# Sums of squares in four column tiles, root and reciprocal on a quarter of the width, and weights split in one piece of 1024 columns

## The chip, the cores and the metric

The kernel runs on one core of a Trainium2 chip. The time is that of the device for one execution, in microseconds (us); before the change it is 1908.05 us, the median of three runs (1899.71 to 1910.66). PE is the matrix engine, DVE the vector engine, ACT the scalar engine, POOL the GpSimd engine and SP the engine that issues the weight transfers.

## The reference, cut to what matters

Two layers work on 528 tokens (512 and 16 meta tokens) of 1024 channels. Each has a token mixer and a channel mixer, and an RMS norm stands before each of them:

```python
def rmsnorm(x, g):
    x32 = x.astype(jnp.float32)
    y = x32 * lax.rsqrt(jnp.mean(x32 * x32, axis=-1, keepdims=True) + EPS)
    return (y * g.astype(jnp.float32)).astype(x.dtype)

for layer in range(DEPTH):                 # DEPTH = 2
    hn = rmsnorm(hs, mix_norm[layer])      # norm 0 (layer 0), norm 2 (layer 1)
    z = hn @ w_in[layer]                   # then the S5 and RG-LRU branches, gates, w_out
    ...
    hn = rmsnorm(hs, ffn_norm[layer])      # norm 1 (layer 0), norm 3 (layer 1)
    # layer 0: dense SwiGLU of 3072 hidden channels; layer 1: top 2 of 8 experts
```

## The kernel before

Activations stand transposed: 128 partitions carry channels, tile `m` of 8 carries channels 128m to 128m+127, and the free axis carries the 528 tokens. Every product is made of three products of float32r halves (high times high, high times low, low times high). Weights arrive in units of 128 x 1024 float32. For the mixers and the dense part (164 units, the "ring" of three buffers `raw`, `wh`, `wl`) SP loads a unit in two halves of 512 columns (`HALVES`), ACT copies each half to `wh` (the high part, L683), DVE subtracts to get `wl` (the low part, L1052), and PE runs 48 matmuls on the unit (`unit`, L1578). The expert part has its own buffers (`mraw`, `mwh`, `mwl`), always in pieces of 1024 columns, and is not touched. Each engine runs its own list in the order in which the code is written; engines wait for each other by semaphores only.

A norm is spread over the engines. ACT squares tile m (`square`, L696). PE multiplies the squares with a 128 x 128 matrix of ones (`add_squares`, L1586), in full float32, so that the sum over channels stands on all 128 partitions of the PSUM tile `side`; each such matmul shows as two records. For norms 1, 2 and 3 `add_squares` of a tile stands between the units of the product before, two tiles late, and the last two stand at its end. Then, in `norm`, ACT loads the table of the square root with a one-column instruction into `warm` (L700), takes the root of all 528 columns into `rs` (L702), DVE takes the reciprocal in place (L1070), and for each tile DVE multiplies `hs`, the norm's weight and `rs` (L1078), ACT makes `xh`, DVE makes `xl`, and PE starts `first_units` (L1608), two weight units interleaved, tile by tile. Norm 3 feeds the router instead (L1780); PE transposes `hs` (L1765) meanwhile. In norms 0 and 2 POOL prepares tables of the S5 branch at the same time; the first of them, `m1t` (L572), is waited for by PE at L1652.

Of the kernel before, what the change touches and what calls it, by code (L numbers as in the profile page):

```python
# [71 lines left out]
RING = 3  # L72
HALVES = ((0, slice(0, UNIT // 2)), (1, slice(UNIT // 2, UNIT)))
U_IN = 28
# [21 lines left out]
def build(nc, xT, W, cols_d, s5p, s5m, wg, rw, rb, fg, out, hs_d, u_d, y_d, xg_d, yg_d):  # L96
    ctx = ExitStack()
    with ctx:
# [24 lines left out]
        def sem(name):  # L123
            return ctx.enter_context(nc.semaphore(name))
# [171 lines left out]
        side_free = [sem("side_free0"), sem("side_free1")]  # L296
        raw_landed = [[sem(f"raw_landed{i}_{h}") for h in range(2)] for i in range(RING)]
        hi_ready = [sem(f"hi_ready{i}") for i in range(RING)]
# [4 lines left out]
        const_ready = sem("const_ready")  # L303
        hs_ready, sq_ready, ss_ready, rms_ready = sem("hs_ready"), sem("sq_ready"), sem("ss_ready"), sem("rms_ready")
        hn_ready, xh_ready, xl_ready = sem("hn_ready"), sem("xh_ready"), sem("xl_ready")
        hs_saved, hs_back = sem("hs_saved"), sem("hs_back")
# [55 lines left out]
        def live(l, x):  # L362

            return x[:, META:T] if l else halves(x)

        def summed(l, pair):

            return pair[:, 0, 0:TR] if l else pair[:, :, 0:TH]
# [48 lines left out]
        def _(sp):  # L417
# [3 lines left out]
            for u in range(RING):  # L421
                for h, cs in HALVES:
                    sp.dma_start(raw[u][:, cs], W[u, :, cs]).then_inc(raw_landed[u][h], 16)
            with sp.Fori(1, UNITS // RING) as it:
                for s in range(RING):
                    for h, cs in HALVES:
                        sp.wait_ge(lo_ready[s], it * 2 + (h - 1))
                        sp.dma_start(raw[s][:, cs], W[it * RING + s, :, cs]).then_inc(raw_landed[s][h], 16)
            for u in range(UNITS // RING * RING, UNITS):
                s, n = use(u)  # L430
                for h, cs in HALVES:
                    sp.wait_ge(lo_ready[s], 2 * n + h - 1)
                    sp.dma_start(raw[s][:, cs], W[u, :, cs]).then_inc(raw_landed[s][h], 16)
            sp.wait_ge(tab_ready2, 1)
# [230 lines left out]
        def _(act):  # L665
# [8 lines left out]
            def split_hi(u, more=0):  # L674

                if isinstance(u, int) and isinstance(more, int) and u + RING * more >= UNITS:
                    return
                s, n = use(u, more)
                if u >= RING:
                    act.wait_ge(unit_done[s], n)  # L680
                for h, cs in HALVES:
# [8 lines left out]
            def square(i, m):  # L690
# [5 lines left out]
                a.activation(hn[:, m, span], hs[:, m, span], ACT.Square).then_inc(sq_ready, 1)  # L696

            def norm(i):
# [62 lines left out]
            def mixer(l):  # L761
# [94 lines left out]
                for m in range(DK):  # L856
                    act.dma_start(hs[:, m, :], (hs_d if l else xT)[:, m, :]).then_inc(hs_back, 16)
                for m in range(DK):
# [19 lines left out]
            def down(u0, e, last):  # L878
                more = e * (U_FF // RING)
                for j in range(FT):  # L880
# [161 lines left out]
        def _(dve):  # L1042
# [11 lines left out]
            def split_lo(u, more=0):  # L1054
                if isinstance(u, int) and isinstance(more, int) and u + RING * more >= UNITS:
                    return
                s, n = use(u, more)
                for h, cs in HALVES:
# [7 lines left out]
            def norm(i):  # L1066
                name, layer = (("mix_norm", 0), ("ffn_norm", 0), ("mix_norm", 1), ("ffn_norm", 1))[i]
                dve.wait_ge(rms_ready, i + 1)
                span = slice(META if i == 3 else 0, T)
                link(v.reciprocal(rs[:, span], rs[:, span]))  # L1070

# [484 lines left out]
        def _(pe):  # L1556
# [7 lines left out]
            def unit(u, jobs, more=0, before=None, sums=None, short=False):  # L1564
# [3 lines left out]
                s, n = use(u, more)  # L1568
                pe.wait_ge(lo_ready[s], n * 2 + 2)
                for n, (k, a, hi, lo, first, last) in enumerate(jobs):  # L1570
# [11 lines left out]
            def add_squares(i, m):  # L1582

                pe.wait_ge(sq_ready, i * DK + m + 1)
                for b, (t0, t1) in enumerate(((META, T),) if i == 3 else ((0, TH), (TH, T))):
                    ins = mm(side[:, b, 0:t1 - t0], ones[:, :], hn[:, m, t0:t1],  # L1586
                             start=m == 0, stop=m == DK - 1)
                if m == DK - 1:
                    ins.then_inc(ss_ready, 1)

            def norm(i):
                if i == 0:
                    pe.wait_ge(const_ready, 1)
                    for m in range(DK):
                        add_squares(i, m)

            def first_units(u, split):

                slots = [use(u + a) for a in range(2)]
                for s, n in slots:  # L1600
                    pe.wait_ge(lo_ready[s], n * 2 + 2)
                for k in range(DK):
# [155 lines left out]
            for l in range(LAYERS):  # L1758
                if l:
# [10 lines left out]
                    for t in range(TB):  # L1770
                        if t == 1:
                            pe.wait_ge(rms_ready, 4)
                        if t >= 2:
                            pe.wait_ge(hs_tok_ready, t - 1)
                        rows_of(hs, t, 1 - t % 2)

                    pe.wait_ge(prep_pool, 16 * 2)
# [249 lines left out]
```

## Time and profile before

| | |
|---|---|
| median of three runs | 1908.05 us |
| the profiled execution | 1904.79 us |
| its span | 1903.3 us |
| mean granted clock of PE, share of full | 0.952 |
| PE busy | 1741.2 us, 91% |
| DVE busy | 1038.6 us, 55% |
| ACT busy | 789.5 us, 41% |
| POOL busy | 469.0 us, 25% |

The span runs from the first to the last instruction. Busy shares are means over stages with different limits. Times in the rows are microseconds from the start of the span; a row of the timeline joins instructions of one kind that stand together and gives their count. PE's granted clock has two levels, 2.4 GHz (1.0) and 1.2 GHz (0.5).

### The profile page before, as it was taken

The numbers are of one execution on the slowest core, as the hardware profiler recorded it, in microseconds if no ns is written. First come the engines' busy times: TensorE is split into PE (matmuls) and PEld (weight loads), VectorE is DVE, ScalarE is ACT, GpSimd is POOL, SyncE is SP. The second block draws the span as 40 slices with busy tenths as digits, with TensorE's granted clock in tenths as the row PEclk, the third lists the DMA queues.
The fourth block names the chain that finished last, engine by engine and source line by source line (L and its number), as shares of the span: only waits on it lengthen the run. The fifth ranks groups of instructions, "written<-read, shape, count | busy, mean of one in ns | idle before, by whom it ended". The sixth has DMA issues, their size and how long they took to land.

```text
span 1903.3 us, 29292 instructions
## 1 busy us (share of the span) xinstructions
PE 1741.2 (91%) x10884; PEld 1556.1 (82%) x10884; DVE 1038.6 (55%) x1453; ACT 789.5 (41%) x1128; POOL 469.0 (25%) x1201
## 2 busy tenths in 40 slices
PE   4799998998999999998898898996999999999993
PEld 4688998998999999998786786875888877877882
DVE  5556553645333233325366545626855766866885
ACT  4234424323222122223343425224744765765773
POOL 5876783002000000003658881001000000000001
PEclk8788998999999999999888999998999999999997
DMA  3521222246322222223512122314975986986994
GB/s 119 105 60 50 60 79 69 81 141 258 114 92 89 89 89 88 88 89 110 112 57 64 59 78 65 113 66 183 412 252 175 338 301 206 343 304 211 347 367 175
DMA packets 123834, 290.28 MB, mean 153 GB/s; under 512 B 31024, under 2 KB 31152, under 8 KB 123584
## 3 DMA queue, kind: packets, MB, share of 16 engines
q1 hardware_dynamic: 90576, 241.38, 36.0%
q0 software_dynamic: 9120, 32.02, 4.7%
q10 hardware_dynamic: 24016, 15.25, 3.8%
q8 instruction: 77, 1.26, 0.3%
q14 instruction: 45, 0.37, 0.1%
HBM read 260.09 MB, written 28.51 MB: 152 GB/s over the span
## 4 chain that ended last, share of the span: by engine, by line
PE 76%; DVE 9%; ACT 5%; issue 5%; DMA 3%; ACTq 2%; SPq 0%; POOL 0%; POOLq 0%; DVEq 0%
PE acc L1578 40%; PE acc L1820 7%; PE acc L1821 7%; PE acc L1822 7%; PE side L1578 2%; PE side L1662 2%; PE acc L1818 2%; PE acc L1819 1%; PE acc L1608 1%; ACTq L827 1%; DMA uu<-u_d 1%; ACT wh L683 1%; PE side L1586 1%; DVE rs L1070 1%; PE side L1866 1%
## 5 line engine op out<-in xcount | busy, mean ns | idle before, releaser
L1578 PE MATMUL acc<-xh,wh 128*128 128x264 f32 (+1 forms) x1600 | 384.0, 310 | 8.2 <-DVE wl L1052 3.8
L1052 DVE TENSOR_TENSOR mwl<-mraw,mwh 128x1024 fp32r<-128x1024 f32 x288 | 337.6, 1220 | 72.5 <-ACT mwh L947 71.7
L1578 PE MATMUL acc<-xl,wh 128*128 128x264 f32 (+1 forms) x1600 | 375.4, 305 | 0.0
L1578 PE MATMUL acc<-xh,wl 128*128 128x264 f32 (+1 forms) x1600 | 373.6, 304 | 0.0
L1052 DVE TENSOR_TENSOR wl<-raw,wh 128x512 fp32r<-128x512 f32 x328 | 217.9, 705 | 268.5 <-ACT wh L683 263.8
L947 ACT ACTIVATE mwh<-mraw 128x1024 fp32r<-128x1024 f32 x288 | 288.3, 1053 | 61.7 <-PE acc L1822 32.3
L1578 PEld LDWEIGHTS acc<-xh,wh 128*128 128x128 f32 x1600 | 262.7, 193 | 29.2 <-issue 13.8
L1578 PEld LDWEIGHTS acc<-xl,wh 128*128 128x128 f32 x1600 | 261.6, 192 | 10.3 <-issue 1.2
L1578 PEld LDWEIGHTS acc<-xh,wl 128*128 128x128 f32 x1600 | 260.8, 192 | 10.2
L683 ACT ACTIVATE wh<-raw 128x512 fp32r<-128x512 f32 x328 | 187.4, 621 | 188.2 <-PE acc L1578 144.5
L1820 PE MATMUL acc<-mwh,xth 128*128 128x512 f32 x432 | 171.1, 396 | 8.4 <-ACT ytok L1013 5.4
L1822 PE MATMUL acc<-mwl,xth 128*128 128x512 f32 x432 | 168.8, 391 | 0.0
L1821 PE MATMUL acc<-mwh,xtl 128*128 128x512 f32 x432 | 168.8, 391 | 0.0
L639 POOL DMA_DIRECT2D yg_d<-ytok x11 | 5.9, 541 | 522.7 <-ACT ytok L1013 519.1
L534 POOL DMA_DIRECT2D gw<-in_wg x4 | 2.2, 565 | 428.0 <-DVE hs L1267 427.7
L1820 PEld LDWEIGHTS acc<-mwh,xth 128*128 128x128 f32 x432 | 81.5, 189 | 28.0 <-issue 11.2
L1822 PEld LDWEIGHTS acc<-mwl,xth 128*128 128x128 f32 x432 | 81.4, 188 | 17.4
L1821 PEld LDWEIGHTS acc<-mwh,xtl 128*128 128x128 f32 x432 | 81.5, 189 | 16.4
L1820 PE MATMUL acc<-mwh,hth 128*128 128x512 f32 x216 | 85.9, 398 | 0.0
L1821 PE MATMUL acc<-mwh,htl 128*128 128x512 f32 x216 | 84.2, 390 | 0.0
L1822 PE MATMUL acc<-mwl,hth 128*128 128x512 f32 x216 | 84.2, 390 | 0.0
L1578 PE MATMUL acc<-fh,wh 128*128 128x264 f32 x384 | 79.3, 288 | 0.0
(379 smaller groups left out, 2943.3 us busy)
## 6 DMA issues: line engine op xcount, KB each, us to landing
mraw<-in_W SPq DMA_DIRECT2D x288, 512.0 KB, 5.4
raw<-in_W SPq DMA_DIRECT2D x328, 256.0 KB, 2.7
xg_d<-zero POOLq DMA_DIRECT2D x15, 512.0 KB, 9.9
yg_d<-ytok POOLq DMA_DIRECT2D x9, 512.0 KB, 3.7
xt<-xg_d POOLq DMA_DIRECT2D x8, 512.0 KB, 8.6
yg_d<-zero POOLq DMA_DIRECT2D x5, 512.0 KB, 20.1
hs<-in_xT SPq DMA_DIRECT2D x8, 264.0 KB, 4.7
u_d<-uperm ACTq DMA_DIRECT2D x8, 264.0 KB, 2.1
```

What stands on the lines that cost most here:

```text
L683: a.activation(wh[s][:, cs], raw[s][:, cs], ACT.Copy).then_inc(hi_ready[s], 1)
L827: act.dma_start(y_d[b * GB:(b + 1) * GB, :, j, :].rearrange("g h c -> h g c"), ys[j * GC:(j + 1) * GC, b % 2, :, :]).then_inc(y_out[b % 2] ...
L947: a.activation(mwh[w][:, :], mraw[j % RAWS][:, :], ACT.Copy).then_inc(wide_hi[w], 1)
L1052: return v.tensor_tensor(out, a, b, op)
L1070: link(v.reciprocal(rs[:, span], rs[:, span]))
L1578: ins = mm(out, w, x[:, t0:t1], start=first and i == 0, stop=last and i == 2)
L1586: ins = mm(side[:, b, 0:t1 - t0], ones[:, :], hn[:, m, t0:t1], start=m == 0, stop=m == DK - 1)
L1662: ins = mm(out4, ident[:, at:at + P], taps[:, :].rearrange("p (g h) -> p g h", g=GB), start=True, stop=True)
L1818: ins = mm(out[0:HALF], hi[:, 0:HALF], mwl[w][:, cols], start=False, stop=False)
L1820: mm(out, hi, mwh[w][:, cols], start=first, stop=False)
L1821: mm(out, lo, mwh[w][:, cols], start=False, stop=False)
L1822: return mm(out, hi, mwl[w][:, cols], start=False, stop=last)
```

## The change

Three things change in the norms. The sums of squares of a tile are no longer made by two matmuls of 264 tokens on all 128 columns of the array, but by four matmuls of 132 tokens with 32 columns of ones each: quarter g of the tokens goes to partitions 32g to 32g+31. Root and reciprocal then work on 132 columns instead of 528. A new step, `spread_inverse`, brings quarter g of the reciprocals back to all partitions with a full-array float32 matmul whose 128 weight columns are all the unit vector of row 32g; its result stands in PSUM, and L1078's multiplication reads it from there. The load of the root's table moves ahead: to the start of the last stretch of units before norms 1, 2 and 3. For norm 3 the quarters are of 128 tokens, and the new matmuls stand after the first of PE's four groups of transposes.

The fourth thing is the split of the ring's units: transfer, high part and low part of a unit are one instruction of 1024 columns each, with one semaphore each.

```diff
-HALVES = ((0, slice(0, UNIT // 2)), (1, slice(UNIT // 2, UNIT)))
...
+        def quarter(i):
+
+            return (T - span_of(i)) // 4
+
+        def spread(i):
+
+            w = 2 * quarter(i)
+            return acc[:, 0, 1, 0:2 * w].rearrange("p (b c) -> p b c", b=2) if i == 3 else side[:, 2:4, 0:w]
...
                 for s in range(RING):
-                    for h, cs in HALVES:
-                        sp.wait_ge(lo_ready[s], it * 2 + (h - 1))
-                        sp.dma_start(raw[s][:, cs], W[it * RING + s, :, cs]).then_inc(raw_landed[s][h], 16)
+                    sp.wait_ge(lo_ready[s], it)
+                    sp.dma_start(raw[s][:, :], W[it * RING + s, :, :]).then_inc(raw_landed[s], 16)
...
-                for h, cs in HALVES:
-                    act.wait_ge(raw_landed[s][h], n * 16 + 16)
-                    a.activation(wh[s][:, cs], raw[s][:, cs], ACT.Copy).then_inc(hi_ready[s], 1)
+                act.wait_ge(raw_landed[s], n * 16 + 16)
+                a.activation(wh[s][:, :], raw[s][:, :], ACT.Copy).then_inc(hi_ready[s], 1)
...
             def norm(i):
-                act.wait_ge(const_ready, 1)
-                a.activation(warm[:, :], ones[:, 0:1], ACT.Sqrt)
+                if i == 0:
+                    act.wait_ge(const_ready, 1)
+                    sqrt_table()
                 act.wait_ge(ss_ready, i + 1)
-                a.activation(live(i == 3, rs[:, :]), summed(i == 3, side[:, 0:2, :]), ACT.Sqrt, scale=1.0 / D, bias=EPS)\
+                w = quarter(i)
+                a.activation(rs[:, 0:w], side[:, 0, 0:w], ACT.Sqrt, scale=1.0 / D, bias=EPS)\
...
-                for h, cs in HALVES:
-                    dve.wait_ge(hi_ready[s], n * 2 + (h + 1))
-                    tt(wl[s][:, cs], raw[s][:, cs], wh[s][:, cs].bitcast(F32), ALU.subtract).then_inc(lo_ready[s], 1)
+                dve.wait_ge(hi_ready[s], n + 1)
+                tt(wl[s][:, :], raw[s][:, :], wh[s][:, :].bitcast(F32), ALU.subtract).then_inc(lo_ready[s], 1)
...
-                link(v.reciprocal(rs[:, span], rs[:, span]))
+                span, w = slice(span_of(i), T), quarter(i)
+                v.reciprocal(rs[:, 0:w], rs[:, 0:w]).then_inc(inv_ready, 1)
+                dve.wait_ge(spread_ready, i + 1)
...
-                    v.scalar_tensor_tensor(out=hn[:, m, span], in0=hs[:, m, span], scalar=g, in1=rs[:, span],
+                    v.scalar_tensor_tensor(out=halves(hn[:, m, span]), in0=halves(hs[:, m, span]), scalar=g, in1=spread(i),
...
-                for b, (t0, t1) in enumerate(((META, T),) if i == 3 else ((0, TH), (TH, T))):
-                    ins = mm(side[:, b, 0:t1 - t0], ones[:, :], hn[:, m, t0:t1],
+                w = quarter(i)
+                for g in range(4):
+                    t0 = span_of(i) + g * w
+                    ins = mm(side[32 * g:32 * g + 32, 0, 0:w], ones[:, 0:32], hn[:, m, t0:t0 + w],
                              start=m == 0, stop=m == DK - 1)
...
+            def spread_inverse(i):
+
+                w = quarter(i)
+                pe.wait_ge(inv_ready, i + 1)
+                for g in range(4):
+                    ins = mm(spread(i)[:, g // 2, g % 2 * w:(g % 2 + 1) * w],
+                             ident[:, 32 * g:32 * g + 1].to_broadcast([P, P]), rs[:, 0:w], start=True, stop=True)
+                ins.then_inc(spread_ready, 1)
```

ACT's list from the last stretch of the dense part to norm 2, before the change (`wh<-raw` is a unit's high part, `hn<-hs` the square of a tile, `rs<-side` the root):

```order
L866 COMPARE_AND_BRANCH
L683 ACTIVATE wh_57<-raw_54 128x512 x2
...
L885 DMA hs_d<-hs 128x3696
L696 ACTIVATE hn<-hs 128x528
L914 DMA hs_d<-hs 128x528
L700 ACT_TABLE_LOAD
L700 ACTIVATE warm<-ones 128x1
L702 ACTIVATE rs<-side 128x528
L708 ACTIVATE xh<-hn 128x528 x8
```

And the same place after it:

```order
L883 COMPARE_AND_BRANCH
L710 ACT_TABLE_LOAD
L710 ACTIVATE warm<-ones 128x1
L693 ACTIVATE wh_57<-raw_54 128x1024
...
L904 DMA hs_d<-hs 128x3696
L706 ACTIVATE hn<-hs 128x528
L933 DMA hs_d<-hs 128x528
L718 ACTIVATE rs<-side 128x132
L724 ACTIVATE xh<-hn 128x528 x8
```

The table load and the one-column instruction moved from between the last square and the root to a place eight units earlier; the root has 132 columns, and a unit's high part is one instruction.

PE's list at norm 3, before the change (L1578 is the last unit, L1765 the transposes of `hs`, L1780 the router's product):

```order
L1578 MATMUL acc<-xl,wh_58 128x512
L1578 MATMUL acc<-xh,wl_61 128x512
L1586 MATMUL side<-hn,ones 128x512 x3
L1765 MATMUL side<-ident,hs 128x128 x32
L1780 MATMUL acc<-hn,rws 8x512 x8
L1784 MATMUL acc<-ident,lgt 128x8 x4
```

And after it (L1626 is `spread_inverse`):

```order
L1597 MATMUL acc<-xh,wl_61 128x512
L1607 MATMUL side<-hn,ones 32x128 x12
L1798 MATMUL side<-ident,hs 128x128 x8
L1626 MATMUL acc<-rs,ident 128x128 x4
L1798 MATMUL side<-ident,hs 128x128 x24
L1815 MATMUL acc<-hn,rws 8x512 x8
```

The three full-array matmuls on the squares became twelve of 32 columns, and the spreading matmuls stand between the first eight transposes and the other 24, which now wait behind them.

## Rows read from the trace of the kernel before

**Rows 1.** The page's part 4: shares of the chain that ended last, by engine.

```profile
PE 76%; DVE 9%; ACT 5%; issue 5%; DMA 3%; ACTq 2%; SPq 0%; POOL 0%; POOLq 0%; DVEq 0%
```

**Rows 2.** Waits of PE: line, waited for: us in total, times, longest.

```profile
PE acc L1608 <- DVE xl L1052: 24.9, 3, 11.7
```

**Rows 3.** Timeline of norm 1: start, length, engine, line, operation, count, idle before.

```profile
444.23 0.64 ACT L696 ACTIVATE hn<-hs 128x528 f32<-128x528 f32 x1 [5.79 <-DVE hs L1231]
444.89 1.28 ACT L700 ACT_TABLE_LOAD   x1
446.30 0.59 ACT L702 ACTIVATE rs<-side 128x528 f32<-128x528 f32 x1
446.92 3.45 DVE L1070 RECIPROCAL rs<-rs 128x528 f32<-128x528 f32 x1 [2.72 <-ACT rs L702]
450.41 1.45 DVE L1078 SCALAR_TENSOR_TENSOR hn<-hs,cols,rs 128x528 f32<-128x528 f32 x2
443.30 2.83 PE L1586 MATMUL side<-hn,ones 128*128 128x264 f32 x12
452.74 0.78 PE L1608 MATMUL acc<-xh,wh 128*128 128x264 f32 x2 [6.62 <-DVE xl L1052]
```

**Rows 4.** Timeline: short forms on DVE and ACT, full-array float32 on PE.

```profile
19.41 0.55 DVE L1295 RECIPROCAL p_rden<-p_den 128x64 f32<-128x64 f32 x1
69.99 0.22 ACT L806 ACTIVATE taps<-side 128x64 f32<-128x64 f32 x1 [4.87 <-PE side L1652]
1140.17 1.99 PE L1662 MATMUL side<-taps,ident 128*128 128x64 f32 x16
```

**Rows 5.** Timeline of PE: two sums of squares between two units.

```profile
868.88 1.05 PE L1586 MATMUL side<-hn,ones 128*128 128x264 f32 x4
870.01 0.40 PE L1578 MATMUL acc<-fl,wh 128*128 128x264 f32 x2
```

**Rows 6.** Timeline of PE at the tiled matmuls L1624, and their weight loads.

```profile
100.50 0.39 PE L1685 MATMUL side<-sr,m2y 128*128 128x66 f32 x2
100.82 1.11 PE L1624 MATMUL side<-xc,gw 64*64 64x264 f32 x8
101.86 0.51 PE L1578 MATMUL acc<-xh,wh 128*128 128x264 f32 x2
102.21 0.41 PE L1578 MATMUL acc<-xl,wh 128*128 128x264 f32 x2
L1624 PEld LDWEIGHTS side<-xc,gw x128: 129/133/228, 100.8 to 1058.2; 64*64 64x64 f32 x128
```

**Rows 7.** Windows (span, busy PE, PEld, DVE, ACT, POOL, clock); timeline of POOL, PE.

```profile
30.10:42.00 11.90, 9.38 (x65) 9.41 (x66) 11.87 (x19) 5.96 (x10) 10.66 (x17) 0.76 0.01 2
43.40:54.50 11.10, 8.68 (x70) 8.26 (x68) 10.38 (x51) 5.92 (x8) 9.13 (x27) 1.00 0.34 113
120.94 0.29 POOL L476 TENSOR_TENSOR pt<-cfi,pbuf 128x64 f32<-128x64 f32 x1
68.09 1.86 PE L1652 MATMUL side<-c,m1t 128*128 128x16 f32 x8 [4.13 <-issue]
```

**Rows 8.** Timeline of PE at the router.

```profile
1291.58 7.03 PE L1780 MATMUL acc<-hn,rws 128*8 128x512 f32 x16 [0.97 <-DVE hn L1078]
```

**Rows 9.** The chain of waits; two stalls of PE in the timeline.

```profile
452.74 13.22 PE acc L1608 x96
410.65 5.85 PE acc L1578 x48
128.34 0.69 PE L1683 MATMUL side<-uu,m 128*128 128x66 f32 x2 [2.44 <-DVE sr L1052]
163.21 0.44 PE L1683 MATMUL side<-uu,m 128*128 128x66 f32 x2 [2.46 <-DVE sr L1052]
```

**Rows 10.** The page's part 5: DVE's low parts in both sizes.

```profile
L1052 DVE TENSOR_TENSOR mwl<-mraw,mwh 128x1024 fp32r<-128x1024 f32 x288 | 337.6, 1220 | 72.5 <-ACT mwh L947 71.7
L1052 DVE TENSOR_TENSOR wl<-raw,wh 128x512 fp32r<-128x512 f32 x328 | 217.9, 705 | 268.5 <-ACT wh L683 263.8
```

More of the change, by code:

```diff
@@ L296, in build @@
         side_free = [sem("side_free0"), sem("side_free1")]
-        raw_landed = [[sem(f"raw_landed{i}_{h}") for h in range(2)] for i in range(RING)]
+        raw_landed = [sem(f"raw_landed{i}") for i in range(RING)]
         hi_ready = [sem(f"hi_ready{i}") for i in range(RING)]
@@ L304, in build @@
         hs_ready, sq_ready, ss_ready, rms_ready = sem("hs_ready"), sem("sq_ready"), sem("ss_ready"), sem("rms_ready")
+        inv_ready, spread_ready = sem("inv_ready"), sem("spread_ready")
         hn_ready, xh_ready, xl_ready = sem("hn_ready"), sem("xh_ready"), sem("xl_ready")
@@ L364, in live, with span_of @@
             return x[:, META:T] if l else halves(x)
+        def span_of(i):
+            return META if i == 3 else 0
+        def quarter(i):
[3 more added lines that the diff above has]
+            return acc[:, 0, 1, 0:2 * w].rearrange("p (b c) -> p b c", b=2) if i == 3 else side[:, 2:4, 0:w]
         def summed(l, pair):
@@ L421, in _ @@
             for u in range(RING):
-                for h, cs in HALVES:
-                    sp.dma_start(raw[u][:, cs], W[u, :, cs]).then_inc(raw_landed[u][h], 16)
+                sp.dma_start(raw[u][:, :], W[u, :, :]).then_inc(raw_landed[u], 16)
             with sp.Fori(1, UNITS // RING) as it:
                 for s in range(RING):
-                    for h, cs in HALVES:
-                        sp.wait_ge(lo_ready[s], it * 2 + (h - 1))
-                        sp.dma_start(raw[s][:, cs], W[it * RING + s, :, cs]).then_inc(raw_landed[s][h], 16)
+                    sp.wait_ge(lo_ready[s], it)
+                    sp.dma_start(raw[s][:, :], W[it * RING + s, :, :]).then_inc(raw_landed[s], 16)
             for u in range(UNITS // RING * RING, UNITS):
                 s, n = use(u)
-                for h, cs in HALVES:
-                    sp.wait_ge(lo_ready[s], 2 * n + h - 1)
-                    sp.dma_start(raw[s][:, cs], W[u, :, cs]).then_inc(raw_landed[s][h], 16)
+                sp.wait_ge(lo_ready[s], n)
+                sp.dma_start(raw[s][:, :], W[u, :, :]).then_inc(raw_landed[s], 16)
             sp.wait_ge(tab_ready2, 1)
@@ L696, in square, with sqrt_table @@
                 a.activation(hn[:, m, span], hs[:, m, span], ACT.Square).then_inc(sq_ready, 1)
+            def sqrt_table():
+                a.activation(warm[:, :], ones[:, 0:1], ACT.Sqrt)
             def norm(i):
-                act.wait_ge(const_ready, 1)
-                a.activation(warm[:, :], ones[:, 0:1], ACT.Sqrt)
+                if i == 0:
+                    act.wait_ge(const_ready, 1)
+                    sqrt_table()
                 act.wait_ge(ss_ready, i + 1)
-                a.activation(live(i == 3, rs[:, :]), summed(i == 3, side[:, 0:2, :]), ACT.Sqrt, scale=1.0 / D, bias=EPS)\
+                w = quarter(i)
+                a.activation(rs[:, 0:w], side[:, 0, 0:w], ACT.Sqrt, scale=1.0 / D, bias=EPS)\
                     .then_inc(rms_ready, 1)
@@ L857, in mixer @@
                     act.dma_start(hs[:, m, :], (hs_d if l else xT)[:, m, :]).then_inc(hs_back, 16)
+                sqrt_table()
                 for m in range(DK):
@@ L879, in down @@
                 more = e * (U_FF // RING)
+                if last:
+                    sqrt_table()
                 for j in range(FT):
@@ L1068, in norm @@
                 dve.wait_ge(rms_ready, i + 1)
-                span = slice(META if i == 3 else 0, T)
-                link(v.reciprocal(rs[:, span], rs[:, span]))
+                span, w = slice(span_of(i), T), quarter(i)
+                v.reciprocal(rs[:, 0:w], rs[:, 0:w]).then_inc(inv_ready, 1)
+                dve.wait_ge(spread_ready, i + 1)
                 def lower(m):
@@ L1568, in unit @@
                 s, n = use(u, more)
-                pe.wait_ge(lo_ready[s], n * 2 + 2)
+                pe.wait_ge(lo_ready[s], n + 1)
                 for n, (k, a, hi, lo, first, last) in enumerate(jobs):
@@ L1592, in norm @@
                 if i == 0:
-                    pe.wait_ge(const_ready, 1)
+                    pe.wait_ge(const_ready, 2)
                     for m in range(DK):
                         add_squares(i, m)
+                if i == 3:
+                    return
+                spread_inverse(i)
+            def spread_inverse(i):
[5 more added lines that the diff above has]
+                ins.then_inc(spread_ready, 1)
             def first_units(u, split):
@@ L1600, in first_units @@
                 for s, n in slots:
-                    pe.wait_ge(lo_ready[s], n * 2 + 2)
+                    pe.wait_ge(lo_ready[s], n + 1)
                 for k in range(DK):
@@ L1775, in _ @@
                         rows_of(hs, t, 1 - t % 2)
+                        if t == 0:
+                            spread_inverse(3)
                     pe.wait_ge(prep_pool, 16 * 2)
```

2 lines of the change are left out of this document (removed).

## The prediction

> **What bounds the kernel now.** I read the chain of waits first: 76% of it is PE, 9% DVE, 5% ACT [rows 1]. So an edit pays where it shortens PE's own list or a stretch in which PE stands still. The waits of PE come next: the longest sum is the first weight units after norms 0 to 2 waiting for DVE's `xl`, 24.9 us in three times [rows 2]. The timeline of norm 1 shows that wait's inside [rows 3]: PE's last sum of squares ends at 443.30 + 2.83 = 446.13 and PE works again at 452.74. Between them stand the rest of the table load, the root (0.59), the reciprocal (3.45, the largest piece), the first multiplications and splits. The reader is to see that all of it is one after the other. The change aims at two places: this stretch, and the sums of squares in PE's list. The split of the ring's units touches ACT and DVE, which mostly wait.
>
> **The stretch in norms 1 and 2.** I go through norm 1; norm 2 has the same list.
> - Table load: it ends at 446.17, and the root follows. The last square ends at 444.87 [rows 3]. Moved ahead, the load costs ACT 1.28 us earlier, covered by idle time such as the 5.79 us before that square; without that cover it would delay one high part by 1.5 us, with nearly two units (5.85 us each, [rows 9]) until PE needs it. The root then waits for the last sums alone. They start at about 444.92, and I give them 0.44 us of steps and 0.28 us of run-out, so the root starts at 445.65 instead of 446.30: -0.65.
> - Root: 0.22 us for 64 columns from PSUM [rows 4], 0.59 for 528 [rows 3]; on the line between them 132 columns take 0.28: -0.31.
> - Reciprocal: 0.55 us for 64 columns [rows 4], 3.45 for 528, so 6.25 ns a column and 0.98 for 132: -2.47.
> - Spreading, which is new and entirely on the path: four full-array float32 matmuls, eight records. Sixteen records of 64 columns took 1.99 us with their run-out, 0.12 each [rows 4]; records of 264 columns come 0.22 apart (four in 1.05 with run-out, [rows 5]). A record of 132 columns has half of the latter's work, 0.11, so the 0.12 of the former counts: 8 x 0.12 = 0.96, and 0.24 for run-out and the two handovers: +1.20. At half clock it would be +2.1.
> - The multiplication reads PSUM instead of SBUF: counted as nothing.
>
> Sum: -2.2 us each, -4.4 for both. The bounds are -1.3 (half clock) and -2.4.
>
> **Norm 0.** PE has been idle there long, so the spreading costs +2.1 and DVE gains only about 0.7 us. What ends last is another thing: PE reaches the S5 branch's first matmul and waits 4.13 us until 68.09 for POOL's table [rows 7]. POOL is slowed by DVE: between 30.10 and 42.00, with DVE in two-operand work from SBUF, it did 17 operations in 11.9 us (0.70 each); between 43.40 and 54.50, 27 in 11.1 us (0.41) [rows 7]. The 17 lost 17 x 0.29 = 4.9 us to 16 large DVE operations, 0.3 each. While DVE multiplied a PSUM operand with one from SBUF, at 120.94, POOL's operation took 0.29 us, its undisturbed length [rows 7]. The eight multiplications of the norm now have their second operand in PSUM, so POOL gains 8 x 0.3 = 2.4 us, and the 4.13 us of waiting can give that. Bounds: 0 and 4.1. I take -2.4. The Trainium skill ("SBUF — State Buffer", in the list of port rules) says that a DVE operation with two SBUF inputs and a GpSimd operation that reads SBUF exclude each other for the whole instruction. The trace agrees with it in the 0.29 us against 0.70. Without it, the first mixer would get norm 0's 0.7 us at most, and the sum would be 1.7 us less.
>
> **Norm 3.** The router's product waits 0.97 us for DVE [rows 8]; that is all that the shorter root and reciprocal can give. The spreading matmuls stand before three groups of transposes that were done under the reciprocal and now come behind it. I take -0.3; bounds -1.0 and +1.0.
>
> **Sums of squares in PE's list.** Of 24 (eight each for norms 1 to 3), 21 stand in PE's stream, three in the stretches above. One costs now: from 868.88 to the second pair of the next unit at 870.01, less one pair's step of 0.24, is 0.89 us [rows 5]. The new one has eight records of 132 columns, 0.11 us of work each. How many run at once no row shows for this form. The nearest is the gate product on tiles of 64 x 64: eight records of 264 columns (0.22 each) took from 100.82 to 101.86, 1.04 us, where one after the other would be 1.76: two at a time. Around them the neighbours stand 0.10 further apart on each side (100.50 to 100.82 for 0.22; 101.86 to 102.21 for 0.25) [rows 6]. So 0.88 us are work and 0.36 are the cost of going to tiles and back. Two at a time, the new form costs 0.44 + 0.36 = 0.80; four at a time 0.22 + 0.36 = 0.58; one at a time 0.88 + 0.36 = 1.24. I take the middle of the first two, 0.69, because there are four tiles here: -0.20 each, -4.2 in all. Bounds: -6.5 and +7.4, and worse if the weight loads count too (below).
>
> **The split in one piece.** Per unit DVE spends 1.22 us instead of two of 0.705, and ACT similarly less [rows 10], but both wait for PE most of the time. Where the split stands in DVE's or ACT's part of the chain (about eight places in the mixers, by the chain of waits) it saves 0.1 us: -0.8. Against it: the low part can only start when the whole high part is done, so the pair ends 0.4 us later where DVE waits. PE's slack of nearly two units covers that; if none did, the eight places would cost +3. A transfer of 512 KB lands later than its first half did; that matters only where a transfer is late.
>
> **Sum.** -4.4 - 2.4 - 0.3 - 4.2 - 0.8 = -12.1 us, against the profiled execution's 1904.79 (span 1903.3, the rest is around it): 1892.7. That execution is one of four, whose median is 1906.4; the three shown have 1908.05. From 1906.4 the sum gives 1894.3. I forecast **1894 us**.
>
> **Rivals.**
> - *More than that* (1889): four tiles at a time give 2.3 us more, and the clock holds. After the stretch of norm 1 the first 96 matmuls take 13.22 us where 96 at full clock take 2 x 5.85 = 11.70 [rows 9]: 1.5 us lost, 3 in two norms. With matmuls in its middle the quiet time falls to about 2.4 us. For it speaks a stall of 2.46 us after which the records have full-clock length (0.44 for two), against it one of 2.44 us after which they have 0.69 [rows 9]. So it is open, and I leave it out of the sum.
> - *The norms' own stretches only* (1901): POOL's gain is lost to another wait before 68.09 or behind it, and a sum of squares costs what it did: 4.4 + 0.3 + 0.8 = 5.5 us of gain. Free waits in the mixers between ACT, DVE and POOL speak for it.
> - *The tiling does not do what it says* (1906): tiles run one after another. 21 x 0.35 = 7.4 us are lost and the other 7.9 gained. Rows 6 speak for pairs only, and cannot tell which two records run together.
> - *Slower: weight loads in line* (1928). If a column tile's load waits for the matmul before it, since all four tiles use all rows, each record costs its load too: 0.13 us [rows 6]. Then a sum of squares takes 8 x 0.24 + 0.36 = 2.28 us, 1.39 more than now, 29 us in 21 places, against 7.9 gained: 1906.4 + 21.3. It decides from 1.27 us for one sum of squares. Against it: in [rows 6] eight loads of 0.13 and eight records of 0.22 took 1.04 us, so loads were hidden, but there the tiles differ in rows. The Trainium skill ("TensorE: Matmul & The Clock Gate", Part 3) says that a weight load overlaps a running matmul only if the row group differs. No run so far shows it for column tiles. The same page reports a gain of 2.38 times for three column tiles, which by itself speaks for the case of several at a time.
>
> **How the numbers follow.** Chances: the forecast 0.41, more 0.20, norms only 0.22, tiles in line 0.09, loads in line 0.08. The measurement tells 0.5% from no change, that is 1898.5 or less against 1908.05. The forecast has its own range of 1888 to 1900 and counts 0.8 as faster, the first rival wholly, the second 0.3: 0.33 + 0.20 + 0.07 = 0.60 faster. Slower are the last rival and a rest: 0.08. The remaining 0.32 is within 0.5%. The range, 1882 to 1907, takes in all but the last rival and the tails.
>
> **What would show it.** Right: a reciprocal of about 1 us; PE back at work 2.2 us sooner after its last sums in norms 1 and 2; the first matmul on POOL's table about 2.4 us earlier than 68.09; a sum of squares that costs PE 0.6 to 0.8 us between units. Wrong: one of 1.2 us or more; spreading matmuls of over 2 us; PE waiting for a unit's low part in the mixers; longer half-clock stretches there.

## The result, and the profile after

The changed kernel takes 1888.48 us (median of eight runs, 1879.06 to 1894.03) where the kernel before, run beside it, takes 1905.72 (eight runs, 1896.55 to 1910.66): a ratio of 0.991, interval 0.9891 to 0.9929, or about 17 us. A second set of runs gave 0.9919 (0.990 to 0.9937), 15 us. The forecast was 1894 with a range of 1882 to 1907. The direction and the range held; the terms behind the sum did worse, as the traces show. The measured median lies on the 1889 of the rival called "more than that".

The profiled execution took 1883.83 us, its span 1882.3 against 1903.3. The page's share of the chain that ended last, by engine, answers to [rows 1]:

```profile
PE 73%; DVE 6%; issue 5%; ACT 5%; POOL 4%; DMA 3%; ACTq 2%; SPq 0%; POOLq 0%; DVEq 0%
```

PE's waits (line, what it waited for: us in total, times, longest) answer to [rows 2]. Before, PE stood 12.5 us for the last squares (the first row below is of the kernel before) and 24.9 for `xl`. The 24.9 are now two pieces, one for the quarter reciprocal and one for the first `xl`; the wait for the squares stays. Norm 0 has the longest wait for the squares and the longest for the reciprocal.

```profile
PE side L1586 <- ACT hn L696: 12.5, 2, 11.9
PE side L1607 <- ACT hn L706: 15.4, 4, 12.6
PE side L1626 <- DVE rs L1088: 13.8, 3, 11.0
PE acc L1641 <- DVE xl L1071: 7.2, 3, 2.4
PE side L1716 <- DVE sr L1071: 7.8, 6, 2.8
```

The timeline of norm 1 (start, length, engine, line, operation, count, idle before) answers to [rows 3]:

```profile
432.20 0.64 ACT L706 ACTIVATE hn<-hs 128x528 f32<-128x528 f32 x1 [5.55 <-DVE hs L1250]
432.90 0.43 PE L1607 MATMUL side<-hn,ones 128*32 128x132 f32 x8 [0.88 <-ACT hn L706]
433.40 0.28 ACT L718 ACTIVATE rs<-side 128x132 f32<-128x132 f32 x1 [0.55 <-PE side L1607]
433.71 0.98 DVE L1088 RECIPROCAL rs<-rs 128x132 f32<-128x132 f32 x1 [1.54 <-ACT rs L718]
434.75 2.13 PE L1626 MATMUL side<-rs,ident 128*128 128x132 f32 x8 [1.41 <-DVE rs L1088]
436.91 1.44 DVE L1097 SCALAR_TENSOR_TENSOR hn<-hs,cols,side 128x528 f32<-128x528 f32 x2 [2.22 <-PE side L1626]
439.24 0.78 PE L1641 MATMUL acc<-xh,wh 128*128 128x264 f32 x2 [2.37 <-DVE xl L1071]
```

The root and the reciprocal have the forecast lengths to the hundredth (0.28, 0.98). The spreading takes 2.13 us, not 1.2.

A sum of squares between two units, and its weight loads, answer to [rows 5]:

```profile
855.17 0.43 PE L1607 MATMUL side<-hn,ones 128*32 128x132 f32 x8
855.88 0.40 PE L1597 MATMUL acc<-fl,wh 128*128 128x264 f32 x2
L1607 PEld LDWEIGHTS side<-hn,ones x256: 106/109/154, 12.5 to 1264.3; 128*32 128x32 f32 x128
```

By the same reckoning as for [rows 5] it costs 855.88 - 855.17 - 0.24 = 0.47 us, where it was 0.89. The eight records span 0.43 us, the last one's run-out with them. With 0.11 us of work each and a length of about 0.28, two at a time would span 0.6; one after the other on the full array such records span 1.06 (sums_full below). So four ran at a time.

Where did the 21.0 us between the two traces come from? Windows of the two kernels over the same stages (span, then busy time and count of PE, PEld, DVE, ACT and POOL, clock, DMA share, GB/s). Before, the first mixer up to the last wait for `y1l`, then the second mixer:

```profile
32.62:327.14 294.52, 262.46 (x1953) 252.82 (x1953) 165.21 (x311) 104.99 (x172) 213.37 (x571) 0.89 0.27 70
891.82:1169.39 277.57, 248.19 (x1472) 215.41 (x1473) 148.76 (x237) 104.59 (x172) 195.38 (x518) 0.92 0.27 72
```

After, the same:

```profile
32.36:317.16 284.80, 254.80 (x1952) 245.98 (x1953) 156.96 (x283) 102.11 (x144) 221.26 (x573) 0.94 0.28 73
875.91:1150.40 274.49, 248.56 (x1473) 216.18 (x1473) 140.80 (x209) 101.84 (x144) 202.09 (x521) 0.92 0.28 73
```

| stage | before | after | less |
|---|---|---|---|
| norm 0 and start | 32.62 | 32.36 | 0.3 |
| first mixer to the wait for `y1l` | 294.52 | 284.80 | 9.7 |
| rest of it, with eight sums of squares | 118.99 | 116.17 | 2.8 |
| norm 1, from the last sum to the first unit | 6.61 | 5.91 | 0.7 |
| dense part, with eight sums | 432.41 | 430.71 | 1.7 |
| norm 2 | 6.67 | 5.96 | 0.7 |
| second mixer to `y1l` | 277.57 | 274.49 | 3.1 |
| rest, norm 3, router | 144.13 | 141.77 | 2.4 |
| experts to the end | 589.78 | 590.13 | -0.3 |

The profiled execution is the second fastest of its eight, 4.6 us under their median, so the 21.0 us are more than the 15 to 17 of the medians.

The largest piece lies where the prediction had only POOL's gain. In the first mixer PE did the same instructions (1953 and 1952), yet was busy 7.7 us less: a granted clock of 0.94 in place of 0.89 (about 0.01 of that is a stretch that the record misses, see the last section). Only 2.1 us less are idle. So three questions were open: what the split and the norms give apart, what the clock does to both, and how much of this stage is chance.

### The profile page after: what moved, and what is told of

The parts are those of the page before. It is cut to its first block, busy times and chain, and to the rows that moved or that the text cites. A ratio compares the mean times of both kernels' runs of the same rounds, so it can differ in the third digit from the quotient of the medians.

```text
span 1882.3 us, 28818 instructions
## 1 busy us (share of the span) xinstructions
PE 1728.1 (92%) x11060; PEld 1541.1 (82%) x11060; DVE 1006.2 (53%) x1289; ACT 772.4 (41%) x964; POOL 481.2 (26%) x1201
## 4 chain that ended last, share of the span: by engine, by line
PE 73%; DVE 6%; issue 5%; ACT 5%; POOL 4%; DMA 3%; ACTq 2%; SPq 0%; POOLq 0%; DVEq 0%
PE acc L1597 38%; PE acc L1855 7%; PE acc L1856 7%; PE acc L1857 7%; PE side L1597 2%; PE acc L1853 2%; PE side L1695 2%; PE acc L1854 2%; PE acc L1641 1%; ACTq L843 1%; DMA mraw<-in_W 1%; DMA uu<-u_d 1%; POOL pt L487 1%; ACT wh L693 1%; PE side L1901 1%
## 5 line engine op out<-in xcount | busy, mean ns | idle before, releaser
L1597 PE MATMUL acc<-xh,wh 128*128 128x264 f32 (+1 forms) x1600 | 379.9, 307 | 5.4 <-DVEq L1253 2.2
L1071 DVE TENSOR_TENSOR wl<-raw,wh 128x1024 fp32r<-128x1024 f32 x164 | 203.5, 1242 | 299.6 <-ACT wh L693 298.9
L693 ACT ACTIVATE wh<-raw 128x1024 fp32r<-128x1024 f32 x164 | 172.2, 1051 | 178.1 <-PE acc L1597 142.5
```

What stands on the lines that cost most here:

```text
L693: a.activation(wh[s][:, :], raw[s][:, :], ACT.Copy).then_inc(hi_ready[s], 1)
L1071: return v.tensor_tensor(out, a, b, op)
L1597: ins = mm(out, w, x[:, t0:t1], start=first and i == 0, stop=last and i == 2)
```

## The experiments

Ratios are to the kernel before in the same set of runs, with 95% intervals. A ratio of 0.001 is 1.9 us. The diffs show the lines that matter; `...` stands for the rest.

**split_only**: the kernel before, with the diff's lines for the split alone.

```diff
-                for h, cs in HALVES:
-                    tt(wl[s][:, cs], raw[s][:, cs], ...)
+                tt(wl[s][:, :], raw[s][:, :], ...)
...
```

> The kernel before with one edit: each unit's transfer, high part and low part in one piece of 1024 columns; norms as before. Theory A (the one piece is nearly neutral: one start less on ScalarE and VectorE, against GpSimd held longer beside each 1024-wide subtraction): within 2 us of the kernel before, and GpSimd's instructions beside such a subtraction take about 1.2 to 1.3 us where they take 0.7 to 0.9 now. Theory B (the 10 us that the first mixer gained come from the split): 8 to 12 us under the kernel before.

Measured: 1895.19 us, 0.9959 (0.9944 to 0.9974), 8 us faster. Theory A is out; theory B has the size, but not the place: the first mixer is 2.7 us shorter, the second 5.6, and there it is idle time. Its second mixer and its waits for `sr` in the whole run:

```profile
890.60:1162.59 271.99, 248.09 (x1473) 216.23 (x1473) 141.75 (x209) 102.27 (x144) 204.71 (x518) 0.91 0.29 74
PE side L1678 <- DVE sr L1048: 4.8, 5, 1.8
```

And the same wait in the kernel before:

```profile
PE side L1683 <- DVE sr L1052: 12.9, 6, 2.8
```

PE is as busy as before (248.1 against 248.2) in 5.6 us less: 29.4 us of idle time became 23.9. PE waits 8 us less for `sr`, which is made on DVE, in the whole run, and DVE does 28 instructions and 7 us less in the stage. Part of it moves to the next wait: the one for `ra`, made on ACT, grows from 5.6 to 10.1 us in the whole run. And as theory A has it for POOL, the first matmul on its table in the first mixer comes later than in the kernel before, at 70.57 against 68.09:

```profile
70.57 0.58 PE L1647 MATMUL side<-c,m1t 128*128 128x16 f32 x2 [6.21 <-issue]
```

**norms_only** and **norms_again**: the changed kernel with the halves back.

```diff
+HALVES = ((0, slice(0, UNIT // 2)), (1, slice(UNIT // 2, UNIT)))
-                tt(wl[s][:, :], raw[s][:, :], ...)
+                for h, cs in HALVES:
+                    tt(wl[s][:, cs], raw[s][:, cs], ...)
...
```

> The changed kernel with the two halves of 512 columns back; norms, column tiles and spreading as changed. Theory A: 14 to 17 us under the kernel before, so within 3 us of the changed kernel; and the first matmul on GpSimd's table in the first mixer starts 1 to 3 us sooner than the changed kernel's 67.87, since GpSimd is no longer held by 1024-wide subtractions. Theory B: 4 to 8 us under the kernel before only.

> The kernel norms_only once more. It came out level with the changed kernel (0.9909 against 0.991 and 0.9919), while the split alone was worth 8 us to the kernel before, low halves alone cost the changed kernel 8 us, and halves cost warm_all 13 us. Theory A (the split is worth something under the new norms too, and the first 0.9909 was the lucky end of how the half-clock stretches fall): a ratio of 0.993 to 0.996. Theory B (the two parts share one gain, and low_halves lost by its own mix): 0.990 to 0.992 again.

Measured: 0.9909 (0.9885 to 0.9933), 1886.64 us, and the second time 0.9938 (0.9919 to 0.9958), 1891.14 us. Theory A held both times. So the norms alone give 12 to 17 us, and between the two sets of one program lie 5 us. Against either of these, the two sets of the changed kernel (0.991 and 0.9919) put what the split adds between -2 and 5 us: its share in the measured gain isn't settled. The table of GpSimd (POOL) came when it was expected. Timeline of PE in norms_only, at the table and at the `sr` of the blocks behind it:

```profile
65.82 0.58 PE L1690 MATMUL side<-c,m1t 128*128 128x16 f32 x2 [5.14 <-issue]
85.44 0.66 PE L1713 MATMUL side<-uu,m 128*128 128x66 f32 x2 [6.79 <-DMA uu<-u_d]
128.44 0.70 PE L1721 MATMUL side<-uu,m 128*128 128x66 f32 x2 [2.49 <-DVE sr L1075]
PE side L1721 <- DVE sr L1075: 13.1, 6, 2.8
```

65.82 is 2.3 us before the 68.09 of [rows 7], and 85.44 still is 2 us ahead of the kernel before (87.42). But at 128.44 PE stands where it stood before, at 128.34 [rows 9]: with halves, the wait for `sr` sets the time, and POOL's gain ends there. With one piece that wait isn't there (PE reaches the same place at 125.86 without idle time), but the table is late.

**low_halves**: transfer and high part in one piece, the low part on DVE in two.

```diff
-                tt(wl[s][:, :], raw[s][:, :], ...).then_inc(lo_ready[s], 1)
+                for h, cs in HALVES:
+                    tt(wl[s][:, cs], raw[s][:, cs], ...).then_inc(lo_ready[s], 1)
...
```

> The changed kernel with the transfer and the high part in one piece of 1024 columns and the low part in two of 512. Theory A (what the one piece gains is starts saved in the S5 chain on ScalarE and VectorE, what it loses is GpSimd's time beside a long subtraction): GpSimd's table in the first mixer is ready about 2 us sooner than the changed kernel's 67.87, and the whole run is within 3 us of the changed kernel, since the VectorE chain gives back 0.2 us per unit. Theory B (a long subtraction does GpSimd no harm): the first mixer's table comes at 67 to 68 as in the changed kernel and the run is 1 to 4 us slower.

Measured: 1895.92 us, 0.9973 (0.996 to 0.9986), against 0.9919 for the changed kernel in the same set: 10 us slower by the ratios and 8 by the medians, more than either theory had, though the table is as early as theory A has it. The table and its waits for `sr`:

```profile
65.64 0.60 PE L1686 MATMUL side<-c,m1t 128*128 128x16 f32 x4 [3.67 <-issue]
PE side L1717 <- DVE sr L1071: 14.8, 6, 3.2
```

With two pieces on DVE alone the waits for `sr` are back (14.8 us; the changed kernel has 7.8), and the run is 8 to 10 us longer. It isn't shown that DVE's instructions alone count: norms_only has the same two on DVE, and the transfer and the high part in two as well, and is 7 to 12 us faster than low_halves by the ratios. What differs is that behind a high part in one piece both low parts wait for the whole of it; no run takes that apart. In the trace the loss stands in the first mixer; the second takes 274.0 us, the changed kernel's 274.5. A long subtraction does hold POOL. In the changed kernel two of POOL's small operations beside one took four times the length of the next:

```profile
60.37 1.32 POOL L579 TENSOR_TENSOR pt<-apr,bx 128x64 f32<-128x64 f32 x1
61.66 1.27 POOL L580 TENSOR_TENSOR pt<-api,by 128x64 f32<-128x64 f32 x1
62.89 0.28 POOL L579 TENSOR_TENSOR pt<-apr,bx 128x64 f32<-128x64 f32 x1
```

**sums_full**: the four quarter sums on the whole array, one after the other into one bank; the weights of a quarter are ones in 32 of 128 columns, zero elsewhere (the identity's zero margin, with 32 ones behind it).

```diff
-                    ins = mm(side[32 * g:32 * g + 32, 0, 0:w], ones[:, 0:32], hn[:, m, t0:t0 + w],
-                             start=m == 0, stop=m == DK - 1)
+                    ins = mm(side[:, 0, 0:w], ident[:, PADW - 32 * g:PADW + P - 32 * g], hn[:, m, t0:t0 + w],
+                             start=m == 0 and g == 0, stop=m == DK - 1 and g == 3)
...
```

> The changed kernel with the same four quarter sums done on the full array: for each quarter a weight tile of 128 columns that is one in 32 of them and zero elsewhere, all four added into the same bank one after the other. The quarter root, quarter reciprocal and spreading stay. Theory A (four tiles run at once, that is where the cheap sums come from): a sum of squares between two units costs 0.9 to 1.1 us again, as the 0.89 before, where it costs about half a microsecond now; with 21 in TensorE's list and one or two at each norm's end the run is 8 to 14 us over the changed kernel. Rival (the gain is in the narrow matmuls or elsewhere, not in tiles at once): under 3 us over the changed kernel.

Measured: 1889.95 us, 0.9928 (0.9909 to 0.9947), so 2 to 3 us over the changed kernel by the ratios. By the time alone that is the rival's number, and theory A's 8 to 14 was missed; the cost of one sum is theory A's:

```profile
864.69 1.06 PE L1608 MATMUL side<-hn,ident 128*128 128x132 f32 x8
865.83 0.40 PE L1598 MATMUL acc<-fl,wh 128*128 128x264 f32 x2
```

That is 865.83 - 864.69 - 0.24 = 0.90 us, as expected: the cheap sum comes from tiles that run at once. The three stages with eight sums each are 119.7, 432.7 and 144.2 us long here, against 116.2, 430.7 and 141.8 with tiles, 7.9 us in all. That agrees with 21 sums at 0.43 us more each, 9 us. Its spreading in norms 1 and 2 ran at full clock (4.9 and 5.1 us from last sum to first unit, against 5.9 and 6.0) and its second mixer is 2 us shorter, but its first mixer is 7.5 us longer, and the whole trace 10.1. This trace is the slowest of its six runs. So the tiles are worth about 8 us where they stand, while the medians show 2 to 3, and with intervals of 0.0019 on each ratio 8 us is at the edge of what they allow. Where the difference goes is open.

**table_late**: the square-root table loaded in the norm again.

```diff
-                if i == 0:
-                    act.wait_ge(const_ready, 1)
-                    sqrt_table()
+                if i == 0:
+                    act.wait_ge(const_ready, 1)
+                sqrt_table()
...
-                sqrt_table()
...
-                if last:
-                    sqrt_table()
```

> The changed kernel with the square-root table loaded in each norm again, right before the root, as in the kernel before. Theory: the load costs 1.28 us and starts when the last square ends, so it ends about 0.4 us after the last sum of squares now that this sum is short; TensorE's stretch in norms 1 and 2 grows by 0.3 to 0.7 us each. Rival: it is hidden as before, and the stretch stays within 0.1 us.

One execution, 1895.76 us. Timeline of its norm 1:

```profile
441.25 1.28 ACT L710 ACT_TABLE_LOAD   x1
441.29 0.43 PE L1604 MATMUL side<-hn,ones 128*32 128x132 f32 x8 [0.89 <-ACT hn L706]
442.65 0.26 ACT L718 ACTIVATE rs<-side 128x132 f32<-128x132 f32 x1
443.98 2.12 PE L1623 MATMUL side<-rs,ident 128*128 128x132 f32 x8 [2.26 <-DVE rs L1085]
```

PE waits 2.26 us for the reciprocal where it waits 1.41 with the early load: 0.85 us a norm, more than either expectation. In the kernel before, the last sum ended at 446.13 and the load at 446.17, so the sum hid it; here the sum ends at 441.72 and the load at 442.53, and the root follows at 442.65.

**keep_warm**: matmuls that nobody reads in norms 1 and 2.

```diff
+            def filler(i, n):
+                if i in (1, 2):
+                    for _ in range(n):
+                        mm(acc[:, 0, 0, 0:P], ones[:, :], ident[:, 0:P], start=True, stop=True)
...
```

> The changed kernel plus matmuls that nobody reads (ones by identity, 128 columns) in norms 1 and 2 alone: three before the last sum of squares, five after it, nine after the spreading. Theory A (the half clock from 434.2 to 444.4 and from 871.1 to 881.3 comes of TensorE's idle time in the norm, and costs there about 1.0 us in the spreading and 2.5 in the units behind it): both stretches go, and the run is 4 to 7 us under the changed kernel. Rival (the fillers fill the gaps but the clock falls all the same, or it falls a little later by what came before): 0 to 3 us slower than the changed kernel.

Measured: 1882.1 us, 0.9878 (0.9854 to 0.9903), 6 to 8 us under the changed kernel by the ratios, as theory A has it. Timeline of its norm 1, and the window around it:

```profile
436.47 1.38 PE L1636 MATMUL acc<-ident,ones 128*128 128x128 f32 x10
437.95 1.17 PE L1627 MATMUL side<-rs,ident 128*128 128x132 f32 x8
438.95 2.17 PE L1636 MATMUL acc<-ident,ones 128*128 128x128 f32 x18
434.00:446.00 12.00, 11.52 (x109) 10.42 (x108) 8.49 (x13) 4.22 (x8) 10.21 (x19) 1.00 0.68 249
```

In the changed kernel the same norm, spreading included, has a clock of 0.62:

```profile
430.80:444.40 13.60, 8.94 (x61) 7.97 (x60) 9.14 (x14) 4.78 (x8) 11.54 (x21) 0.62 0.72 265
```

At full clock the spreading takes 1.17 us, the forecast's 1.20. The half clock cost about 1 us in it and more in the units behind. The chain of waits has the first 96 matmuls behind norm 1, in the changed kernel and in keep_warm:

```profile
439.24 14.25 PE acc L1641 x96
441.49 11.90 PE acc L1649 x96
```

The kernel before took 13.22 us for them [rows 9].

**after_again**: the changed kernel once more.

> The changed kernel once more, to see what its 1888.48 and its trace vary by. Two profiled executions showed that of the 21 us between the two traces about 5 stand in how much of the first mixer fell on half clock. Theory: the stage from 32 to 317 us takes 285 to 293 us this time, norm 1's stretch 4.9 (full clock in it) or 5.9 us (half clock), and the median is within 3 us of 1888. Rival: the first mixer's 284.8 us repeat to within 1 us, which would make the 10 us gained there an effect of the change.

Measured: 1887.44 us, 0.9919 (0.99 to 0.9937). The first mixer took 286.8 us, with a clock of 0.93: the theory's 285 to 293 holds, and it isn't the repeat to within 1 us of the rival. Two other kernels do exactly what the changed kernel does up to the end of this stage, since their edits stand behind it: keep_warm and table_late. So there are four traces of the same work: 284.8 us (the changed kernel), 286.8, 288.8 (keep_warm) and 294.0 (table_late). The second and the last:

```profile
31.48:318.29 286.81, 256.31 (x1953) 247.50 (x1953) 156.78 (x283) 102.12 (x144) 220.18 (x573) 0.93 0.28 72
31.43:325.39 293.96, 260.35 (x1952) 251.09 (x1953) 156.19 (x283) 102.34 (x144) 217.06 (x573) 0.90 0.27 70
```

They spread over 9 us, the longer the lower the clock (0.94, 0.93, 0.92, 0.90), and the kernel before, with one trace, had 294.5. So the 9.7 us of this stage aren't shown to come from the change: some of it may, how much no trace tells. The others lie in the same band or near it: 291.8 (split_only) and 292.3 (sums_full), and with halves 291.4 and 293.2 (norms_only twice) and 297.6 (low_halves).

**warm_all**: keep_warm, and such matmuls before the other long waits.

```diff
+                    if (l, b, part) in ((0, 0, 0), (1, 3, 0), (0, 0, 1), (1, 0, 1)):
+                        free((k + 1) % 2, a0 + (k + 1) // 2)
+                        fill((k + 1) % 2, 20)
...
+                    if g == 0:
+                        fill(0, 20)
...
+            fill(0, 30)
             pe.wait_ge(pick_ready, 1)
...
```

> The kernel keep_warm, plus matmuls that nobody reads ahead of TensorE's other long waits: 20 each (0.24 us each at full clock) before the first block's two waits and the merge units' wait for y1l in the first mixer, before the fourth block's wait for ra, the first block's for uu and y1l in the second, and 30 before the wait for pick. Theory A (each such wait costs 3 to 5 us of half clock behind it, on the path): 5 to 15 us under keep_warm's 1882. Theory B (in the mixers the other engines set the pace, so a faster TensorE only waits longer): within 4 us of keep_warm, with fewer half-clock stretches and more idle time.

Measured: 1869.41 us, 0.9831 (0.9809 to 0.9853), 9 us under keep_warm and 17 under the changed kernel of the same set, by the ratios: theory A held. It is the fastest of all but for warm_more, which is level with it. The mean clock rose from 0.960 in the changed kernel to 0.977, with a span of 1866.8 us. Its second mixer:

```profile
874.00:1140.00 266.00, 253.66 (x1585) 221.74 (x1584) 142.49 (x207) 104.44 (x146) 204.22 (x517) 0.97 0.30 75
```

The three that followed take it apart.

**warm_before**: the kernel before with those matmuls and nothing of the change; 25 behind the last sum in norms 1 and 2, in keep_warm's place.

```diff
+                if l == 0:
+                    fill(0, 25)
...
```

> The kernel before, without any part of the change, plus matmuls that nobody reads: 25 behind the last sum of squares of norms 1 and 2, and the ones that warm_all has before TensorE's long waits in the mixers and before pick. It tells how much of warm_all's 1869.41 needs the change. Theory A (the half clock behind each stall is a cost of its own): 14 to 22 us under the kernel before, so about 1884, since warm_all lies 18 under the changed kernel. Theory B (the change is what lets a fuller TensorE pay): under 8 us.

Measured: 1889.26 us, 0.9926 (0.9897 to 0.9955), 14 us faster, the low end of theory A.

**warm_more**: also in norm 0 and before the first mixer's fourth block.

```diff
-                filler(i, 5)
+                fill(0, {0: 40, 1: 5, 2: 5, 3: 0}[i])
...
```

> warm_all plus 40 such matmuls before and 9 behind the spreading of norm 0 and 20 before the fourth block's wait in the first mixer. Theory A: the first units behind norm 0 run at full clock (they took 0.42 us for records of 0.30 until 37.8 us), which saves 2 to 4 us; the fourth block's another 0 to 4: 1863 to 1868. Theory B (GpSimd's table and the S5 chain set the first mixer's pace): the first mixer keeps its length within 2 us.

Measured: 1869.01 us, 0.9817 (0.9794 to 0.9841): level with warm_all. Its first mixer takes 285.4 us where warm_all's takes 287.0, so theory B's length holds; which engine sets the pace there isn't shown by that.

**warm_halves**: warm_all with halves.

```diff
+HALVES = ((0, slice(0, UNIT // 2)), (1, slice(UNIT // 2, UNIT)))
...
```

> warm_all with the units' split in two halves of 512 columns again. With the clock mostly held, the comparison of one piece with halves no longer hangs on where half-clock stretches fall. Theory A (with the new norms the split is worth little): within 3 us of warm_all's 1869. Theory B (it is worth the 8 us that it gave to the kernel before): 5 to 9 us above.

Measured: 1882.58 us, 0.9882 (0.9856 to 0.9908), 10 us over warm_all by the ratios and 13 by the medians, so at or beyond the top of theory B. The intervals leave room for the 8 us that one piece gave alone. Taken one by one, the idle-filling matmuls (0.0074), the norms (0.0062 to 0.0091) and the split (0.0041) sum to 0.018 to 0.021; together they gave 0.0169. warm_halves has three waits for `sr` in each mixer, 5.9 and 7.1 us in all, and half clock follows the long ones at 123.49 and 994.24.

## Why the prediction was right, and where it was wrong

- **Norms 1 and 2 (-2.2 each).** Counted from the end of the last square (444.87, now 432.84) to PE's first unit, the stretch went from 7.87 to 6.40 us: -1.5. The pieces: start of the root 1.43 to 0.56, -0.87 (forecast -0.65); root -0.31 and reciprocal -2.47, as forecast; from the reciprocal's end to the multiplication 0.04 to 2.22, +2.2 (forecast +1.20). The failed piece is the spreading's clock. The +2.1 at half clock was named there as a bound and was the value. With a held clock the forecast is met: in keep_warm the stretch is 5.44 us, 2.4 less. Counted from PE's last sum, as under "What would show it", it is only 0.7 less (6.61 to 5.91), because that sum itself ends sooner. And the first units behind norm 1, which the sum left alone, got 1.0 us slower (13.22 to 14.25), those behind norm 2 0.6: about half of the gain went back there.
- **Norm 0 (-2.4 by POOL).** The mechanism held and the gain came, with halves: the first matmul on the table came 2.3 and 2.4 us earlier, and POOL's operations beside a multiplication with a PSUM operand took 0.32 us. Two things failed. In the changed kernel the long subtractions took back most of it in one trace and half in the other (67.87 and 67.01, against 68.09), which was nowhere counted: the split was weighed on DVE and ACT, not on POOL, though the same rule says it. And the step "the 4.13 us of waiting can give that" took a wait for the end of the chain: in norms_only the wait for `sr` behind it ended at the old time.
- **Norm 3 (-0.3).** From the first transposes to the router 5.29 us before (1286.29 to 1291.58) and 5.63 after (1264.61 to 1270.24): +0.3, inside its bounds. The spreading in the line of transposes costs what the wait gave.
- **Sums of squares (-4.2).** Mis-sized. One costs 0.47 us, not 0.69, and lies below the lowest bound of 0.58: four tiles run at once, and going to tiles and back costs by my estimate 0.47 - 0.22 = 0.25 us, not the 0.36 of the 64 x 64 tiles. 21 x 0.42 = 8.8 us. The rival of weight loads in line fell: the Trainium skill's rule ("TensorE: Matmul & The Clock Gate", Part 3), that a load overlaps only another row group's matmul, doesn't fit the 0.43 us in which eight loads of 0.109 and eight matmuls went by, all on the same rows.
- **The split (-0.8).** The worst term: 8 us alone, though on top of the new norms between -2 and 5. The step that failed is "both wait for PE most of the time". It is true on average and false in the S5 chain, where DVE is what PE waits for: `sr` cost 12.9 us with halves and 4.8 without, of which the wait for `ra` took 4.5 back. The count of "about eight places" by the chain of waits counted instructions that stood in the chain, not the DVE work queued before the one awaited.
- **The clock.** It was left out of the sum, and in the rival called "more" it was 3 us. That rival named the measured time (1889) and had four tiles at a time right, but the clock didn't hold in the norms: 0.62 there, and the units behind got slower. Most of the first mixer's 9.7 us is the clock, and how it falls differs by 9 us between traces of the same work. Filling idle time alone gave the kernel before 14 us.

Of the four signs for "right", one came: the reciprocal of 0.98 us. PE was back 0.7 us sooner instead of 2.2, the first matmul on POOL's table came 0.2 us sooner (1.1 in the second trace) instead of 2.4, and a sum cost 0.47 instead of 0.6 to 0.8. One of the signs for "wrong" came as well, a spreading of over 2 us.

So the sum of 12.1 was near the measured 15 to 17 by luck in part: terms missed to both sides, sums of squares and split too small, norms and POOL too large. What held is the main mechanism, shorter sums of squares and a shorter chain in the norms.

## What to carry to other kernels

Before pricing an edit at nothing because its engine is idle most of the time, look in PE's waits for the ones that name this engine, and ask what else stands in its queue in those stretches; in the kernel before, one piece in place of two was worth 8 us, ten times the forecast. When a gain upstream is priced by the wait it shortens, follow PE to the next wait and see whether that one moves too. And when PE must wait for some microseconds, matmuls that nobody reads are worth a try: here they gave 14 us with no other change. And before a stage's gain in one trace is put down to a change, compare traces of kernels that do the same work up to there: here they differ by 9 us.

## What was not expected of the hardware

- Matmuls of float32 on four column tiles of 32 start 7 ns apart, in two groups about 0.13 us apart; eight records took 0.43 us and the next unit followed 0.36 us after their start.
- From 27.87 us the changed kernel's spreading took 2.13 us, the length that it has at half clock, while the window shows a granted clock of 1.00; the kernel before shows 0.60 there. Here the recorded clock misses a stretch near the start of the span, and the lengths of the records are what to go by:

```profile
27.87 2.13 PE L1626 MATMUL side<-rs,ident 128*128 128x132 f32 x8 [10.97 <-DVE rs L1088]
27.00:38.00 11.00, 7.76 (x34) 7.49 (x34) 8.74 (x14) 3.86 (x6) 9.33 (x22) 1.00 0.26 94
```

- Two sets of runs of one program (norms_only, norms_again) gave 0.9909 and 0.9938. For parts of a change below 5 us, the stages of the traces tell more than the medians.
